# A skipped expert loop with a shorter body, and a LayerNorm with one modulation unit per wait

## The reference

```python
cond = jax.nn.silu(c) @ w_ada + b_ada          # shifts, scales and gates: 14 x 1024 columns
for layer in range(2):
    h = modulate(x, shift, scale)
    y = mlstm_layer(h, ...)  if layer == 0 else moba_layer(h, ...)   # attention, keys and values from shared_kv
    x = layer_norm(ALPHA * x + gate * y, ln_g[layer, 0], ln_b[layer, 0])
    h = modulate(x, shift, scale)
    y = moe_ffn(h, ...)      # 16 experts, 2 per token, each (silu(h @ Wg) * (h @ Wu)) @ Wd with 512 hidden columns
    x = layer_norm(ALPHA * x + gate * y, ln_g[layer, 1], ln_b[layer, 1])
```

## Time and profile before

| what | before |
| --- | --- |
| median of 3 runs | 2435.8 us |
| the profiled execution's own time | 2435.83 us |
| its span | 2434.0 us |
| TensorE busy, share of the span | 2276.6 us, 94% |
| TensorE's share of the chain that ended last | 83% |
| "issue" in that chain | 2.2% |
| mean granted clock | 0.978 |
| instructions in the trace | 33290 |

### The profile page before, as it was taken

One profiled execution on the slowest core, in us unless ns is written; L12 is line 12 of the kernel. 1 busy time (PEld: TensorE's weight loads), 2 busy tenths in 40 slices (PEclk: granted clock), 3 DMA queues, 4 the chain that ended last, 5 costly groups with the idle time before them and its releaser, 6 DMA issues.

```text
span 2434.0 us, 33290 instructions
## 1 busy us (share of the span) xinstructions
PE 2276.6 (94%) x12894; PEld 1743.6 (72%) x12894; DVE 1247.4 (51%) x2278; ACT 950.9 (39%) x1702; POOL 113.8 (5%) x96
## 2 busy tenths in 40 slices
PE   5999998998899899969999899999999999899999
PEld 4877774454477444448878679888888886698887
DVE  4624534111323511147763666677677636666776
ACT  2532202111222211145544665654454446645543
POOL 1000000000000000000005200000000052000000
PEclk9999999999999999989999999999999999899999
DMA  9975439999721899946653415466566525054663
GB/s 355 321 235 206 156 135 406 429 429 425 283 104 70 369 428 430 427 132 188 196 189 114 166 45 199 120 208 191 155 195 194 193 95 183 26 184 139 204 185 95
DMA packets 310256, 535.68 MB, mean 220 GB/s; under 512 B 14894, under 2 KB 200944, under 8 KB 296304
## 3 DMA queue, kind: packets, MB, share of 16 engines
q1 hardware_dynamic: 309180, 532.61, 60.7%
q10 hardware_dynamic: 948, 1.28, 0.2%
HBM read 532.81 MB, written 1.05 MB: 219 GB/s over the span
## 4 chain that ended last, share of the span: by engine, by line
PE 83%; DVE 8%; ACT 3%; DMA 3%; issue 2%; SPq 1%; ACTq 0%; DVEq 0%
PE bank L593 15%; PE bank L1046 14%; PE bank L875 13%; PE yacc L909 9%; PE bank L880 7%; PE bank L577 4%; PE yacc L788 2%; PE yacc L610 2%; PE bank L628 2%; PE bank L1264 1%; PE bank L657 1%; PE yacc L1058 1%; PE bank L986 1%; PE yacc L1208 1%; PE bank L750 1%
## 5 line engine op out<-in xcount | busy, mean ns | idle before, releaser
L1428 ACT ACTIVATE arena<-bank 128x256 f32<-128x256 f32 (+3 forms) x382 | 146.7, 407 | 585.6 <-PE bank L593 126.8
L875 PE MATMUL bank<-h_split,w_hi 128*128 128x512 f32 x1408 | 352.3, 392 | 0.0
L2321 DVE TENSOR_TENSOR w_lo<-wring,w_hi 128x1024 fp32r<-128x1024 f32 x264 | 307.3, 1218 | 10.7 <-ACT w_hi L1649 10.7
L1649 ACT ACTIVATE w_hi<-wring 128x1024 fp32r<-128x1024 f32 x264 | 277.5, 1056 | 49.0 <-PE yacc L909 49.0
L875 PEld LDWEIGHTS bank<-h_split,w_hi 128*128 128x128 f32 x1408 | 259.3, 189 | 50.0
L880 PEld LDWEIGHTS bank<-h_split,w_lo 128*128 128x128 f32 x1408 | 193.4, 191 | 20.4 <-DVE h_split L2363 5.5
L880 PE MATMUL bank<-h_split,w_lo 128*128 128x256 f32 x1408 | 199.5, 284 | 5.3 <-DVE h_split L2363 5.3
L2900 POOL TENSOR_TENSOR wx_lo<-wring,wx_hi 128x1024 fp32r<-128x1024 f32 x42 | 107.3, 2557 | 1947.5 <-ACT wx_hi L1468 1947.5
L1046 PE MATMUL bank<-wring,arena 128*64 128x512 f32 x768 | 172.3, 603 | 15.8 <-issue 8.3
L1046 PE MATMUL bank<-arena 128*64 128x512 f32 x672 | 169.7, 599 | 10.1 <-issue 6.3
L1661 ACT ACTIVATE H<-bank 128x256 f32<-128x256 f32 x176 | 67.4, 383 | 252.4 <-PE bank L880 250.5
(11 more groups left out here) (403 smaller groups left out, 3814.6 us busy)
## 6 DMA issues: line engine op xcount, KB each, us to landing
wring<-in_ffn_w_in SPq DMA_DIRECT2D x176, 512.0 KB
wring<-in_w_ada SPq DMA_DIRECT2D x28, 2048.0 KB
wring<-in_ffn_w_out SPq DMA_DIRECT2D x88, 512.0 KB
wring<-in_w_in SPq DMA_DIRECT2D x20, 2048.0 KB
wring<-in_moe_w_gate SPq DMA_DIRECT2D x16, 2048.0 KB, 21.5
wring<-in_moe_w_up SPq DMA_DIRECT2D x16, 2048.0 KB, 21.2
wring<-in_moe_w_down SPq DMA_DIRECT2D x16, 2048.0 KB, 22.6
arena<-in_moe_w_down SPq DMA_DIRECT2D x12, 2048.0 KB, 20.2
```

The lines of the kernel that those rows point to most:

```text
L875: return mm(b[:, :], r(w_hi[:, j % 2, g, c * HB:(c + 1) * HB]), r(h_split[:, c, :, :].rearrange("p a t -> p (a t)")), start=start, stop=st ...
L1428: ins = f(dst, bank_of(name)[0:dst.shape[0], 0:T] if src is None else src, func, **kw)
L1649: f(w_hi[:, j % 2, part, :].bitcast(F32R), wring[:, u % WSLOTS, part * DC * HB:(part + 1) * DC * HB], ACT.Copy).then_inc(w_hi_ready[part], 1)
L2321: tt(w_lo[:, j % 2, part, :].bitcast(F32R), wring[:, (u0 + j) % WSLOTS, part * DC * HB:(part + 1) * DC * HB], w_hi[:, j % 2, part, :], ALU ...
```

## The change

On the general path TensorE's loop no longer runs over experts with four blocks written out, but over the 64 blocks, each of 24 calls; the weights of a block (a quarter of each of the three matrices) are loaded by SyncE block by block, which makes 12 loads per expert out of 3, once written out for the first expert and once in the loop. In `ln01` the four units are spread: unit 0 ahead of the mean, its turn and unit 1 between mean and variance, unit 2 and the turn of unit 1 behind the variance; unit 3 and the turn of unit 2 follow the value product `bv0`, the turn of unit 3 follows `bv1`. ScalarE's program follows in the same order, and the load of unit 3 moves behind that of `bv0`.

```diff
 def layer_norm(tag):                          # TensorE
     if tag == "ln01":
         ada_unit(units[0])
-        ada_unit(units[1])
     column_sums(f"{tag}.mean", X, DC, sum_ready)
...
     elif tag == "ln01":
         ada_turn(units[0])
-        ada_turn(units[1])
+        ada_unit(units[1])
     column_sums(f"{tag}.var", SQ, DC, squared)
...
     elif tag == "ln01":
         ada_unit(units[2])
-        ada_unit(units[3])
+        ada_turn(units[1])
...
-with pe.Fori(0, NE) as e:                     # TensorE, general(), reached only with the flag set
-    pe.wait_ge(over_landed[l], e * 48 + 48)
-    for n in range(blocks):
-        for g in range(2):
-            for k in range(DC):
-                last = mm(bank[1][:, g * T:(g + 1) * T], w[g][:, k, n * HB:(n + 1) * HB], H[:, k, :], ...)
-        last.then_inc(over_up[l], 1)
-        pe.wait_ge(over_hid[l], e * blocks + n + 1)
-        for m in range(DC):
-            last = mm(ysum(m), wd[:, n, m * P:(m + 1) * P], hid_o, ...)
-        last.then_inc(over_down[l], 1)
+with pe.Fori(0, NE * (FE // HB)) as i:
+    pe.wait_ge(over_landed[l], i * 48 + 48)
+    for g in range(2):
+        for k in range(DC):
+            last = mm(bank[1][:, g * T:(g + 1) * T], w[g][:, k, :], H[:, k, :], ...)
+    last.then_inc(over_up[l], 1)
+    pe.wait_ge(over_hid[l], i + 1)
+    for m in range(DC):
+        last = mm(ysum(m), wring[:, 2, m * P:(m + 1) * P], hid_o, ...)
+    last.then_inc(over_down[l], 1)
...
     if n == 0:                                # TensorE, moba(), behind the value product bv{n}
-        for a in ADA_NORM["ln01"][2:4]:
-            ada_turn(a)
+        ada_unit(ADA_NORM["ln01"][3])
+    ada_turn(ADA_NORM["ln01"][2 + n])
...
-    expert(slice(0, 1))                       # SyncE, under its If
-    with sp.Fori(1, NE) as e:
-        sp.wait_ge(over_down[l], e * (FE // HB))
-        expert(bass.ds(e, 1))
+    for n in range(blocks):
+        if n:
+            sp.wait_ge(over_down[l], n)
+        block(slice(0, 1), n)
+    with sp.Fori(1, NE) as e:
+        for n in range(blocks):
+            sp.wait_ge(over_down[l], e * blocks + n)
+            block(bass.ds(e, 1), n)
...
-for a in ADA_NORM["ln01"]:                    # SyncE, the order of the loads
+for a in ADA_NORM["ln01"][0:3]:
     ada(a)
 for n in range(2):
     load(f"bv{n}", ...)
+    if n == 0:
+        ada(ADA_NORM["ln01"][3])
```

More of the change, by code:

```diff
@@ L1111, in general @@
                     last.then_inc(over_filled[l], 1)
-                w = [wring[:, n, 0:DC * FE].rearrange("p (k n) -> p k n", k=DC) for n in range(2)]
-                wd = wring[:, 2, 0:FE * D // P].rearrange("p (k n) -> p k n", k=FE // P)
-                blocks = FE // HB
-                with pe.Fori(0, NE) as e:
-                    pe.wait_ge(over_landed[l], e * 48 + 48)
-                    for n in range(blocks):
-                        for g in range(2):
-                            for k in range(DC):
-                                last = mm(bank[1][:, g * T:(g + 1) * T], w[g][:, k, n * HB:(n + 1) * HB], H[:, k, :],
-                                          start=(k == 0), stop=(k == DC - 1))
-                        last.then_inc(over_up[l], 1)
-                        pe.wait_ge(over_hid[l], e * blocks + n + 1)
-                        for m in range(DC):
-                            last = mm(ysum(m), wd[:, n, m * P:(m + 1) * P], hid_o, start=False, stop=False,
-                                      skip_group_check=True)
-                        last.then_inc(over_down[l], 1)
+                w = [wring[:, n, 0:DC * HB].rearrange("p (k n) -> p k n", k=DC) for n in range(2)]
+                with pe.Fori(0, NE * (FE // HB)) as i:
+                    pe.wait_ge(over_landed[l], i * 48 + 48)
+                    for g in range(2):
+                        for k in range(DC):
+                            last = mm(bank[1][:, g * T:(g + 1) * T], w[g][:, k, :], H[:, k, :],
+                                      start=(k == 0), stop=(k == DC - 1))
+                    last.then_inc(over_up[l], 1)
+                    pe.wait_ge(over_hid[l], i + 1)
+                    for m in range(DC):
+                        last = mm(ysum(m), wring[:, 2, m * P:(m + 1) * P], hid_o, start=False, stop=False,
+                                  skip_group_check=True)
+                    last.then_inc(over_down[l], 1)
             def attention(tag, heads, q_of, k_of, v_of, before=None, after=None):
@@ L1549, in layer_norm @@
                     ada(units[0])
-                    ada(units[1])
                 squares(centered)
@@ L1555, in layer_norm @@
                     ada_turned(units[0], 0)
-                    ada_turned(units[1], 1)
+                    ada(units[1])
                 evac(f"{tag}.var", nrm[:, 0, :], func=ACT.Sqrt, scale=1.0 / D, bias=eps_ln[:, :])
@@ L1567, in layer_norm @@
                     ada(units[2])
-                    ada(units[3])
+                    ada_turned(units[1], 1)
                 elif tag == "ln10":
@@ L1731, in _ @@
                 if n == 0:
-                    ada_turned(ADA_NORM["ln01"][2], 2)
-                    ada_turned(ADA_NORM["ln01"][3], 3)
+                    ada(ADA_NORM["ln01"][3])
+                ada_turned(ADA_NORM["ln01"][2 + n], 2 + n)
             def projected(it):
@@ L2750, in moe, with block @@
                     sp.wait_ge(*moe_unit_used(l, PAIRS * PAIR_UNITS - 1))
[L2752 to L2755, removed]
-                                .then_inc(over_landed[l], 16)
-                    expert(slice(0, 1))
+                    blocks = FE // HB
+                    def block(one, n):
+                        for g, src in enumerate(mats_over[0:2]):
+                            sp.dma_start(wring[:, g, 0:DC * HB].rearrange("p (k n) -> p k n", k=DC),
+                                         src[:, one, :, n * HB:(n + 1) * HB].rearrange("p e k n -> p (e k) n")) \
+                                .then_inc(over_landed[l], 16)
+                        sp.dma_start(wring[:, 2, 0:D].rearrange("p (k n) -> p k n", k=1),
+                                     mats_over[2][:, one, n:n + 1, :].rearrange("p e k n -> p (e k) n")) \
+                            .then_inc(over_landed[l], 16)
+                    for n in range(blocks):
+                        if n:
+                            sp.wait_ge(over_down[l], n)
+                        block(slice(0, 1), n)
                     with sp.Fori(1, NE) as e:
-                        sp.wait_ge(over_down[l], e * (FE // HB))
-                        expert(bass.ds(e, 1))
-                    sp.wait_ge(over_down[l], NE * (FE // HB))
+                        for n in range(blocks):
+                            sp.wait_ge(over_down[l], e * blocks + n)
+                            block(bass.ds(e, 1), n)
+                    sp.wait_ge(over_down[l], NE * blocks)
             def ffn(w_in, w_out):
```

## The result

| | before | after |
| --- | --- | --- |
| median | 2435.77 us (6 runs, 2435.09 to 2443.53) | 2423.3 us (6 runs, 2421.25 to 2426.69) |
| ratio | | 0.9936, 95% interval 0.992 to 0.9952 |
| span of the profiled execution | 2434.0 us | 2420.8 us |
| mean granted clock | 0.978 | 0.977 |

The forecast was 2422.8 us with a range of 2420 to 2430, and a chance of 0.53 for a gain of more than 0.5%. The gain is 0.64%. Two of the six runs before lie at 2442.2 and 2443.5 us, the other four at 2435.1 to 2435.8, and the median is one of the four.

The account below looks back on a forecast made before the run. TensorE, busy 94% of the span, was taken as the bound, with time to gain only where its chain stands still: 2435.83 us - 6.5 (layer 0) - 6.5 (layer 1) = 2422.8 us, range 2420 to 2430.

Parts of the forecast that it names:

- The experts' path is not entered; what changes is the jump.: Experts' path in both layers: edited code is jumped over; TensorE's skipping branch, 6162 and 6242 ns, is what can change.
- A jump of 1.8 blocks lands beyond the prefetched block, one of 0.66 in it.: TensorE's jump over the general path: 1.8 code blocks before, 0.66 after, landing in the same or next block; both stalls go.
- Rival 2: TensorE's two jumps: both still cost 6 us because a forward jump drops loaded code; 2436 us, no change; chance 0.10.
- rival 1: TensorE's two jumps: one still misses the loaded code, leaving one gain of 6.5 us, 2429.3 us; chance 0.08.
- 0.2 us for the near jump.: TensorE's branch under the If: 0.2 us in each layer, taken from its back-edges, hidden beside 2.15 us of queued scatter matmuls.
- Layer 0: -6.5.: Layer 0, behind the last scatter: value product starts 8.3 us earlier, unit 3 behind it adds 1.8; net -6.5 us.
- Layer 1: -6.5.: Layer 1, behind the scatter: the mean's column sums end at about 1051.5 instead of 1058.10 us, so -6.5 us.
- The reordering's own share is +0.5 to -0.2 us.: Layer 0's ln01: the new unit order by itself changes the time by +0.5 to -0.2 us, the jump about -7.
- The successor is asked for at the jump and can be used 6.2 us later; cover 2 us.: Layer 0, after the jump: the landing block's successor arrives 2 us before TensorE needs it; if that fails, 0.7 us lost.
- no packet within 4 us of the branch: Sign of being right: TensorE's code queue brings no packet within 4 us after the branch in answer to it.
- SyncE's longer body costs nothing.: SyncE's skipped body grows from 6 DMAs to 24; layer 0's branch would lie under a 9.1 us slot wait: zero cost.
- Rival 3, a loop of TensorE that lies in three blocks refetches.: TensorE's swiglu loops: only two blocks kept, so a shifted loop pays some 6.5 us per back-edge; 2443 us; chance 0.03.

Follow-up runs that it names:

- jump_only: The changed kernel with the reordering in and behind ln01 taken back, the block-by-block general path kept: 2420.76 us, ratio to before 0.9937; repeated at 2422.78 us.
- order_only: The kernel before with only the reordering of ln01, its general path left as it was: 2440.72 us, ratio to before 1.0011; repeated at 2439.01 us.
- long_skip: Changed kernel with 205 never-reached instructions more in TensorE's skipped body: 2428.25 us; the pair's other adds 70 waits at TensorE's program start: 2430.65 us.
- no_general: The changed kernel without its If on any engine, the general path left out: 2426.8 us, ratio to before 0.9953.
- edge: The changed kernel with 76 never-reached instructions more in TensorE's skipped body, so 250 are jumped over: 2428.4 us, ratio to before 0.9966.
- changed: The whole change measured again, on another set's chip: 2424.21 us, ratio to before 0.9947; a third time 2422.11 us, ratio 0.9936.

## Why the prediction was right, point by point

- *The experts' path is not entered; what changes is the jump.* Right: jump_only has the whole gain, order_only none to speak of (0.3 us in layer 0's stretch).
- *A jump of 1.8 blocks lands beyond the prefetched block, one of 0.66 in it.* Right, and shown by the pair of long_skip kernels and not only argued. Rival 2 (a forward jump drops what is loaded) falls with the first short branch, rival 1 with the second.
- *0.2 us for the near jump.* Too low: 0.32 and 0.37, so the sign "0.2 us or less, twice" was not met. The price came from a backward branch, and the forward ones take longer. It lies under the scatter, as forecast, so nothing hangs on it: the stretches of no_general are equal.
- *Layer 0: -6.5.* Measured -6.33. Unit 1.85 for 1.79; the idle time ahead of the value product 1.06 for 1.2. *Layer 1: -6.5.* Measured -6.78: the clock did not fall, and the mean took 3.47 us, not the 3.67 of the working.
- *The reordering's own share is +0.5 to -0.2 us.* The one step of the sum's account that failed: it is +1.0. The sum that I made did hold the loss (the variance starts 0.8 later and 1.2 us are idle behind it), but the share was read off the idle times of the two orders without setting the old order beside the short jump; doing that, as for jump_only, gives 7.3 less 6.5, so 0.8 (the expectation of jump_only has 0.9). The total was right because only the share was wrong. The old order fits the two waits better: two turns (1.04 us) in one of 1.5, two units (3.57) in one of 3.5. It also made the loads closer: the value matrix was 0.9 us ahead of its use there.
- *The successor is asked for at the jump and can be used 6.2 us later; cover 2 us.* Right: a packet in 621 to 624 and no stall, and 6.25 us from branch to use in edge. My list of signs was at odds with this, as it wanted no packet within 4 us of the branch; the working was right and the sign wrong. Edge shows what stands behind the cover: 5.9 us, not the 0.7 that I gave for the case that it fails. That price was mis-sized: 0.7 is what was left of the fetch when 25 records at the low clock ran ahead of it. With a landing 14 instructions ahead of the border instead of some 90, only 5 records do, and the clock falls too.
- *SyncE's longer body costs nothing.* Right: its branch took 45 and 59 ns, and its wait for a slot in layer 0 is 9.1 us after, as before.
- *Rival 3, a loop of TensorE that lies in three blocks refetches.* Falls. Counted from the same border, the first swiglu loop lies in three blocks in before and order_only and in two in after and jump_only. The packets say the same: during its first pass (up to the branch at 1154.1 before, 1142.1 after) two came before and one after, here in 1122 to 1160 and in 1110 to 1142 us:

```profile
q8 instruction: 2, 0.03, 0.3%
...
q8 instruction: 1, 0.02, 0.2%
```

The taken back-edges are 207 to 228 ns in all four, and no packet comes in the passes that follow (the earlier trace rows and the row of after). So the loop in three blocks ran again without a fetch. The Trainium skill's "Only 2 cache lines" (Advanced Engine Details and Errata, ISA Cache) does not hold for this engine here, while "128KB on TensorE" in the same list leaves room for more: the measurement decides.

The forecast lay 0.8 us on the faster side of the 0.5% bound. Of the three measurements of the changed kernel two have a ratio of 0.9936 and one 0.9947, and all three intervals hold the bound of 0.995: a split not far from even between faster and no change fits them. That the median came within 0.5 us of the forecast is partly luck: the sum was taken over the two changed stretches, and the unchanged ones move by several us from profile to profile.

## What to carry to other kernels

Code that never runs still costs at the branch that skips it: look at the branch instructions' own durations, and keep a skipped body under about one block of 256 instructions, by rolling it into a loop. That is not enough by itself: edge skips some 250 instructions, both its jumps hit, and it loses 5.9 us. Where the landing falls counts as much as whether the jump hits: leave a good part of a block behind it. What the rolled loop and its smaller loads cost when the general path is entered was not measured, as these inputs never enter it. And a filler is worth placing only where its length fits the wait; two orders with the same work differed by 1 us, which only stretches between landmarks of the trace could tell, not the medians.

## What the hardware showed that I had not expected

- A short forward branch of TensorE took 318 to 450 ns and a taken back-edge 207 to 228 ns, against 45 to 72 ns on the engines with short bodies.
- A jump beyond the loaded code took 6.16 to 6.76 us seven times, in four of these kernels, and 4.33 us once.
- TensorE stood still for 3.2 us behind a jump that hit.
- A loop of TensorE's that lies in three blocks of code ran its later passes without a packet.
- In stretches of unchanged code 7 us more at the low clock went with 3 us more of time (changed against long_skip and edge), and two profiles of the same kernel with the same low time differed by 2.3 us.
